# Weight loads of the hybrid encoder trunk: blocks of four units in a ring of two, in place of blocks of two in a ring of four

## The reference

```
h = layer_norm(x)
for i in range(2):
    proj = h @ w_in[i]                      # 3396 columns: dq dk dv sq sk sv iq ik iw
    a = rms_norm(diff_attention(dq, dk, dv))      # 4 heads, two softmax maps each
    b = indexed_sparse_attention(sq, sk, sv, iq, ik, iw)   # 8 heads, the 64 best keys of each query
    h = layer_norm(ALPHA * h + concat(a, b) @ w_out[i])
    q = h @ peer_wq[i]                      # 8 heads x 2 halves of 128
    # each head: top 16 of 128 keys in both halves, top 16 of the 256 sums -> 128 experts a token
    r = ALPHA * h + sum_k softmax(best)_k * gelu(u[expert_k] . h) * v[expert_k]
    r = r + sigmoid(r @ ple_wg[i] + ple_bg[i]) * (p[i] @ ple_wp[i])
    h = layer_norm(r)
```

## Time and profile before

| | |
|---|---|
| median of 3 runs | 1690.74 us |
| the profiled execution | 1689.92 us, of it the span 1688.1 us |
| TensorE matmul busy | 1254.6 us, 74% |
| VectorE / ScalarE / GpSimd busy | 63% / 27% / 34% |
| moved by DMA | 668.26 MB, 396 GB/s over the span |

### The profile page before, as it was taken

How to read it: one execution, slowest core, us unless ns; L and a number is a source line. 1 busy time by engine, 2 the same in 40 slices (tenths; PEclk the granted TensorE clock), 3 DMA queues, 4 the chain that set the end, 5 groups by cost and what they waited for, 6 DMA issues and landing times.

```text
span 1688.1 us, 17853 instructions
## 1 busy us (share of the span) xinstructions
PE 1254.6 (74%) x6232; PEld 576.2 (34%) x6232; DVE 1070.1 (63%) x2754; ACT 464.2 (27%) x1270; POOL 573.7 (34%) x516
## 2 busy tenths in 40 slices
PE   8978958686787798685766979677766875555556
PEld 6656723231442274132431337232432221001012
DVE  1448679664679764745768694674667877555553
ACT  1323213242223323422222422251122242111112
POOL 0004333334333322343334242343324344444440
PEclk9999978998989999698997989798988997777789
DMA  6769999999999999999999999999999989999992
GB/s 246 289 249 402 421 421 420 421 421 422 421 421 404 416 406 421 421 421 421 421 420 415 405 415 422 421 417 421 421 419 417 372 344 423 421 422 421 422 421 111
DMA packets 93145, 668.26 MB, mean 396 GB/s; under 512 B 10352, under 2 KB 10992, under 8 KB 12288
## 3 DMA queue, kind: packets, MB, share of 16 engines
q0 software_dynamic: 73728, 536.90, 76.9%
q1 hardware_dynamic: 19152, 130.10, 19.1%
q10 hardware_dynamic: 176, 0.13, 0.0%
HBM read 666.04 MB, written 1.05 MB: 395 GB/s over the span
## 4 chain that ended last, share of the span: by engine, by line
DMA 40%; PE 33%; DVE 16%; ACT 4%; issue 3%; POOL 3%; ACTq 0%; POOLq 0%; DVEq 0%
DMA rows<-uv_dram,rows_of 40%; PE acc L1253 12%; PE bank L1042 8%; DVE rows L1002 8%; PE bank L1056 7%; POOL rows L494 3%; ACT dg L666 2%; PE bank L1230 1%; PE bank L1161 1%; PE bank L1032 1%; PE bank L1051 1%; ACT gel L662 1%; PE bank L1153 1%; DVE i L733 0%; DVE i L724 0%
## 5 line engine op out<-in xcount | busy, mean ns | idle before, releaser
L494 POOL DMA_INDIRECT rows<-uv_dram,rows_of x512 | 573.5, 1120 | 1073.4 <-PE acc L1253 856.2
L1002 DVE CUSTOM_DVE_ANT_0 rows<-rows,hx 128x1024 f32<-128x1024 f32 x512 | 620.0, 1223 | 476.7 <-DMA rows<-uv_dram,rows_of 475.1
L1253 PE MATMUL acc<-rows,dg 128*32 128x512 f32 x2048 | 614.6, 730 | 400.9 <-ACT dg L666 400.9
L1253 PEld LDWEIGHTS acc<-rows,dg 128*32 128x32 f32 x2048 | 114.5, 122 | 806.2 <-ACT dg L666 564.7
L662 ACT ACTIVATE gel<-dots 128x2 f32<-128x2 f32 x256 | 51.9, 203 | 894.5 <-DVE dots L1002 894.1
L1042 PEld LDWEIGHTS bank<-xT,wring 128*128 128x128 f32 x2112 | 246.8, 197 | 36.7 <-issue 30.4
L1042 PE MATMUL bank<-xT,wring 128*128 128x128 f32 x2112 | 255.8, 282 | 2.8 <-ACT xT L509 1.1
L1056 PE MATMUL bank<-wring,xT 128*128 128x512 f32 x384 | 173.1, 599 | 1.4 <-ACT xT L509 1.4
L666 ACT ACTIVATE dg<-idg,gel 128x32 f32<-128x32 f32 x512 | 136.6, 314 | 24.6 <-ACT gel L662 1.1
L1056 PEld LDWEIGHTS bank<-wring,xT 128*128 128x128 f32 x384 | 70.7, 190 | 97.6 <-issue 95.6
L662 ACT ACT_TABLE_LOAD x44 | 56.5, 1283 | 0.9
(11 more groups left out here) (156 smaller groups left out, 872.7 us busy)
## 6 DMA issues: line engine op xcount, KB each, us to landing
wring<-wmix_dram SPq DMA_DIRECT2D x96, 1024.0 KB, 9.9
wring<-wclose_dram SPq DMA_DIRECT2D x15, 1024.0 KB, 9.4
rows<-uv_dram,rows_of POOLq DMA_INDIRECT x512, 13.6
rows<-wmix_dram SPq DMA_DIRECT2D x4, 1024.0 KB, 12.7
wring<-wmix_dram SPq DMA_DIRECT2D x4, 512.0 KB, 7.7
rows<-prm_dram SPq DMA_DIRECT2D x2, 1024.0 KB, 10.5
kept<-wmix_dram SPq DMA_DIRECT2D x2, 1024.0 KB, 10.4
fixed<-fixed_dram SPq DMA_DIRECT2D x1, 576.0 KB, 8.3
```

The source lines that it names most:

```text
L494: pool.indirect_dma_start(out=rows[:, slot, :], out_offset=None, in_=uv_d[phase // TILES], in_offset=bass.IndirectOffsetOnAxis(ap=rows_of[ ...
L1002: V.tensor_tensor_reduce(out=rows[:, s, 0:D], in0=rows[:, s, 0:D], in1=hx[:, c, :], scale=1.0, scalar=0.0, op0=ALU.mult, op1=ALU.add, accu ...
L1253: ins = MM(acc[BT * c:BT * c + BT, 512 * i:512 * i + 512], dg[:, s, :], rows[:, s, D + 512 * i:D + 512 * i + 512], start=False, stop=False ...
```

## The change

Blocks hold up to four units instead of two, and the ring has two blocks instead of four. The ring has room for eight units as before, and the bytes loaded are the same. A whole block has 16 KB to a partition in one piece of DRAM (the index block has three units, 12 KB; sub-keys and the per-layer embedding two, 8 KB). The blocks of the output projection hold the units of `mix0a` and `mix1a`, and of `mix0b` and `mix1b`; those of `peer_wq` hold the two heads of groups 0 and 1, of group 2, of group 3 and of group 4. `EXTRA` has two blocks: the whole of group 2 in slots 4 and 5 of `rows`, the whole of group 3 in slots 6 and 7. No instruction of TensorE, VectorE or ScalarE is added or moved.

```diff
-WRING = 4
+WRING, BLOCK = 2, 4
-MIX_BLOCKS = [(u, u + 1) for u in range(0, U_IK, 2)] + [(U_IK,)] + [(u, u + 1) for u in range(U_V, MIX_UNITS, 2)]
-CLOSE_BLOCKS = [(u, u + 1) for u in range(0, CLOSE_UNITS, 2)]
+MIX_BLOCKS = [(U_IQ, U_IQ + 1, U_IK)] + [tuple(range(u, u + 4)) for u in (0, 4, U_SQ, U_SQ + 4, U_V, U_V + 4)]
+MIX_BLOCKS += [(u, u + 1, u + 4, u + 5) for u in (U_WO, U_WO + 2)]
+MIX_BLOCKS += [tuple(range(u, u + 4)) for u in range(U_WQ, U_SK, 4)] + [(U_SK, U_SK + 1)]
+CLOSE_BLOCKS = [(0, 1, 2, 3), (4, 5, 6, 7), (8, 9)]
...
-EXTRA = [tuple(units_of(part)) for part in ("pq1a", "pq2a", "pq2b", "pq3a")]
+EXTRA = [tuple(units_of(f"pq{g}a") + units_of(f"pq{g}b")) for g in (2, 3)]
...
-        wring = sb("wring", [128, WRING, 2 * D])
+        wring = sb("wring", [128, WRING, BLOCK * D])
...
-            return wring[:, slot, :] if slot < WRING else rows[:, EXTRA_SLOT + slot - WRING, :]
+            if slot < WRING:
+                return wring[:, slot, :]
+            at = EXTRA_SLOT + 2 * (slot - WRING)
+            return rows[:, at:at + 2, :].rearrange("p a d -> p (a d)")
...
                         if EXTRA_SLOT <= k < RING:
-                            pool.wait_ge(*block_done[WRING + k - EXTRA_SLOT, 0])
+                            pool.wait_ge(*block_done[WRING + (k - EXTRA_SLOT) // 2, 0])
```

More of the change, by code:

```diff
@@ L276, in count_uses @@
                 w += 1
-            for half, k in enumerate(block):
-                unit[run.key, k] = (*place, half)
+            for at, k in enumerate(block):
+                unit[run.key, k] = (*place, at)
     for k in range(CLOSE_UNITS):
@@ L1021, in unit @@
             def unit(run, k):
-                slot, before, half = UNIT[run.key, k]
+                slot, before, at = UNIT[run.key, k]
                 pe.wait_ge(block_landed[slot], 16 * (before + 1))
-                return place_of(slot)[:, D * half:D * half + D]
+                return place_of(slot)[:, D * at:D * at + D]
             def transposes(run, names, src, waits=None):
@@ L1276, in in_blocks @@
     def in_blocks(units, blocks):
-        return np.stack([np.concatenate([units[b[0]], units[b[-1]]], axis=1) for b in blocks])
+        return np.stack([np.concatenate([units[b[min(i, len(b) - 1)]] for i in range(BLOCK)], axis=1) for b in blocks])
     w_in, w_out, peer_wq, peer_subkeys = a(w_in), a(w_out), a(peer_wq), a(peer_subkeys)
```

## The result

The changed kernel takes 1702.63 us (median of 4 runs, 1701.33 to 1707.54), the one before 1690.80 in the same comparison: ratio 1.0075, 95% interval 1.0054 to 1.0096, so 9 to 16 us slower. Two more comparisons on other chips gave 1.0075 (1.0062 to 1.0088) and 1.0058 (1.0036 to 1.0081). The profiled execution took 1701.33 us, its span is 1699.7.

The account below looks back on a forecast made before the run. From the first gather on, time is bytes over 421 GB/s plus unfilled DMA; before phase 1, TensorE and its weights count. Terms 9.8 - 1.25 + 0.8 - 3.5 + 1.5 - 2.5 = +4.9 us on a 1690.7 median: 1695.6, range 1687.5 to 1705.

Parts of the forecast that it names:

- main case: Whole kernel: the summed terms give 1695.6 us, within 1692 to 1701; chance 0.46.
- the slower rival: Weight loads inside phases and g1 in phase 4 become waits of TensorE: 1711, half of it 1703; chance 0.15.
- The hole: Phase 1: gathers 6 and 7 wait for pq3b, leaving the DMA queue empty and not made good: +9.8 us, bounds 8 to 10.
- the 1.25 us loaded ahead: Before phase 1: the next run's index block lands whole, moving 0.52 MB ahead of the full stretch: -1.25 us.
- Phase 0: Loads of dk and sk, now whole blocks, land later and stall TensorE 0.6 and 0.4 us: +0.8, bounds 0 and 3.
- The ends of phases: Gate weights g1 load after ple, moving bytes into unfilled DMA: -3.5 us, bounds -5.6 and +3.
- Packets: Weight loads: 16 KB per partition goes as one packet, 7424 fewer packets: -2.5 us, of 0 to -4.1.
- Weights inside a phase: TensorE stalls 1 to 3 us per block, free while gathers are queued: +1.5 us, bounds 0 and 20.
- The filled hole: Rival: phase 1's hole opens, but phase ends give 5.6 and packets 4.1 us: -1.2, 1689.5; chance 0.26.
- the faster ones: Two rivals: phase ends take two blocks (1687.5 or less), or fewer loads save fixed cost (1534); together 0.13.

Follow-up runs that it names:

- hole_on_before: The kernel before, with only gathers 4 and 5 of phase 1 made to wait for pq2b, 6 and 7 for pq3b: 1701.77 us against 1693.24, ratio 1.0047.
- after_third: The changed kernel unaltered, timed again beside packets8_again on one chip: 1703.10 us, ratio 1.0058 against the kernel before.
- packets8_again: The kernel of packets8 measured again, on the same chip as the changed kernel (after_third): 1706.08 us, ratio 1.0080 against the kernel before.
- packets8: The changed kernel with each block's halves apart in DRAM, so a partition's 16 KB come as two 8 KB packets: 1705.73 us, ratio 1.0072 against the kernel before.

## Why the forecast was right in kind and short in size

The forecast was 1695.6 in a range of 1687.5 to 1705.0, slower as the likeliest; measured 1702.63. On the profiled executions +4.9 was forecast and +11.4 came (1701.33 - 1689.92), more than twice as much. That the time lies inside the range is owed to its width of 17.5 us: by the forecast's own shares, 1702.63 stands outside the 1692 to 1701 of its main case and in the 1701 to 1712 of the slower rival, to which it gave 0.15.

- *The hole: right.* 9.8 forecast; 10.4 by the rates of the changed kernel, 10.1 between the means of its three executions and the two of before, 9.5 from first to last gather in hole_on_before. Issue and release were as foretold: gather 6 comes 25.3 us behind the first (forecast 24.8), released by pq3b.
- *First to last gather as a whole: near.* The terms 9.8 - 1.25 - 3.5 + 1.5 - 2.5 gave +4.1; measured +4.9 in the pair of profiled executions, +6.1 between the means of three and two. The DMA's unfilled time from first to last gather, by 421 GB/s, rose from 23.1 to 29.7 us between the same means; less the 1.25 us loaded ahead that is +5.3 and leaves little for anything else.
- *Phase 0: the step that failed.* "+0.8; bounds 0 and 3" was 6.5 us in the profiled execution, more than twice the upper bound. Over the executions whose run 0 goes through the ring in twos (six) the first gather goes out at 126.8 on average (124.98 to 129.50), over the six with whole blocks at 133.3 (130.81 to 135.86): 6.6. Two things were mis-sized: the landing was taken from the faster of two blocks (5.2 us) plus 2.5; the mean of the two (6.3) would have given 8.8, and 8.5 and 9.4 came: 3.8 us of waits, of which 2.9 arrived. And no term stood for TensorE's clock, though with whole blocks it ran lower more often: sk0 took 5.4 us in place of 3.74 in four of the six executions with whole blocks, in none of the others, and the second half of the output projection with pq0a took 15.8 us on average in place of 14.5 (14.8 to 16.3 against 13.2 to 15.5).
- *The ends of phases: right in sum.* In the pair of profiled executions phases 2 and 4 gave back 1.0 and 2.9 us (forecast at most 1.3 and 2.5) and phase 3 lost 1.5: -2.4 together. But phase 3 differs as much between executions of one kernel: with wider stretches (390 to 500, 780 to 860 and 1210 to 1270 us behind the first gather) 1.9 and 3.8 us are unfilled in the two of before, 4.6, 1.7 and 1.9 in the three of the changed kernel. Between the means it is -0.9, -0.1 and -2.9, so -3.9 for -3.5, nearly all of it in phase 4.
- *Packets: whole, as assumed; unsettled in time.* The weights' packets took 18.6% of 1699.7 = 316.1 us of each of the 16 engines, against 19.1% of 1688.1 = 322.4 before: some 6 us less, 1 more or less by the rounding, where 2.5 was taken and 4.1 was the bound for the full part alone. How much of it arrives isn't settled; the medians of after_third and packets8_again differ by 3.0.
- *Weights inside a phase: more than forecast, and not by the path foreseen.* TensorE waited 5.6 us for wmix behind the first gather (9.4 in all less 3.8), and the DMA was full at each of them (419 to 428 GB/s in the 10 us around each). What cost was a load that goes out too late to fill a pause of the gathers, with no wait of TensorE: around sk1 and dv0 of phase 1 (160 to 200 us behind the first gather) the three executions of the changed kernel have 1.7, 2.4 and 3.9 us unfilled, the two of before 0.1 each, and 980 to 1050 us behind the first gather 0.0, 2.7 and 2.2 against 0.5 each. With the means that is +3.7 for +1.5.
- *Rivals.* The filled hole and the faster ones are out by hole_on_before. Of the slower rival, in whose range the time lies, the mechanism is right and the place wrong: waits for whole blocks cost time ahead of phase 1, where no gather covers them; inside the phases TensorE's waits don't show as a cost.

The Trainium skill ("DMA: Bandwidth & Descriptors", Anatomy of one DMA) gives its fixed cost of about 2.0 us for transfers that GpSimd issues; these loads are SyncE's. By that rule the kernel with 58 fewer loads should have gained much; the trace shows no such gain, since the chain has no such waits, and the time rose. By the same page of the Trainium skill (Why small descriptors are slow) the packets are worth 1.3 us, as an estimate. The trace has some 6 us less of packet time, and by the 3.0 us between the medians of after_third and packets8_again the time tells neither 1.3 from 4.1 nor either from nothing.

## What to carry to other kernels

When the DMA is full, ask of a change in buffering just two things: does it leave the queue empty anywhere, and what has to be moved inside the full stretch; a hole of 10 us cost 8 to 10 us, while 5.6 us of TensorE's waits inside the full stretch showed no cost. Loads fill the pauses between gathers too, and a coarser block can come too late for one. A coarser ring of the same size halves the cover of each load, and that is paid where nothing else keeps the chip busy: keep the start fine-grained, or put into borrowed buffers what is used first. Price a wait of TensorE with the mean landing time of the row, not the best, and leave room for matmuls at a lower clock.

## What the runs showed of the hardware

- The clock that TensorE gets in 90 to 120 us differs between executions of the same code: 16 matmuls of the output projection took 7.13 us in one execution of the kernel before and 9.23 in another, which still had its first gather 0.7 us sooner. Over kernels whose phase 0 loads alike the first gather moved from 124.98 to 129.50 us.
- Packets of 16 KB beside gathers of 8 KB packets shorten a 2 MB load from 13.8 to 11.5 us to landing (packets8 against the changed kernel), with the same blocks and waits. The gathers' packets took the same, 76.0% of a span of 1706.7 us and 76.4% of 1699.7 (1297 and 1299 us), and their median from issue to landing was 13.3 and 13.4 us; it was 13.0 and 13.3 in the two executions that ran on one chip (packets8_again, after_third).
- A packet of 16 KB costs its engine little less than two of 8 KB: the weights' queue took 316.1 us of each engine with the large ones and 18.9% of 1706.7 = 322.6 with the small ones, for the same 130.09 MB.
